# Triangular inverse of a gated DeltaNet layer: two chunks in each matmul, and two TensorE groups a level in place of three

## The chip, the cores and the metric

The kernel runs on one core of a Trainium2 chip. A core has TensorE (PE: matmuls from SBUF into PSUM), VectorE (DVE), ScalarE (ACT), GpSimd (POOL), SyncE (SP, which issues loads) and DMA queues. The engines run their own instruction streams and meet at semaphores. The metric is the device time of one execution in microseconds (us), lower is better.

## The reference, cut to what matters

One decoder layer on x of 1024 tokens by 1024 features, in float32: RMSNorm, one input projection, sliding-window attention (12 heads) beside a gated DeltaNet (8 heads of 128), sigmoid gates and an output projection, then a SwiGLU feed-forward. The change touches one step of the DeltaNet:

```
a = where(strict, beta_i * (k_i . k_j) * decay_ij, 0)      # strictly lower triangular, per chunk
sol = triangular_solve(eye + a, [beta * v, beta * exp(gc) * k], unit_diagonal)
u_bar, w = sol[..., :dv], sol[..., dv:]
# then a loop over the chunks that carries the state
```

The reference uses chunks of 64 tokens; the kernel uses eight chunks of 128 tokens, and forms the inverse of (eye + a) itself, which it then multiplies with both right-hand sides.

## The kernel before

**Dense stream.** The layer's projections are a long row of dense steps. `dense_k` (its matmul is line L198) issues three 128x512 matmuls for one slice of 128 input features, because each float32 operand is split into a high and a low part. A head's four projections (q, k, v, z) are 64 dense steps, numbered j = 0 to 63, sixteen for each weight tile. POOL splits a weight tile into its parts (L184, then L186) when the tile's slot is free, which is when PE has finished an earlier tile (steps 15, 31, 47, 63).

**Side steps.** The DeltaNet work of head h-1 is laid by hand between the dense steps of head h: `STEPS_AT` says after which dense step each piece is issued, and `delta_iteration` walks j on every engine, so that each engine has the same order. Seven such rounds run as a loop (`delta_heads`, heads 0 to 6 as side work); the eighth (`delta_end`) lies between the first 64 dense steps of the gates, whose outputs ACT takes with L920. On DVE the convolution of the next head's projections shares the round: `TAPS_AT` places its taps (`conv_vec`: L1458 for the first tap, L1460 for the others). ACT takes projection outputs into `conv_in` every eighth step (L1406) and applies SiLU at steps 30, 46 and 58 (`silu_delta_act`, L1416).

**The inverse.** `inv` holds, for each of eight chunks, the inverse of the diagonal blocks found so far; `inv_t` is its transpose, needed because the stationary operand of a matmul must be given transposed; `neg_a` is the masked minus a, transposed (the trace calls it `row`, by its buffer). Steps t00 and t01 (L1183) make the 2x2 blocks. Levels 1 to 6 double the block size, from 2 to 64 = 1 << level columns. A level has three steps, each in two halves of four chunks:

- y (L1194): for each chunk, neg_a times the left half-columns of `inv` (64 moving columns), into bank Y0 or Y1; ACT copies the result to `half_way` (L1292).
- d (L1204): for each chunk, inv times that (64 moving columns), into bank Z0 or Z1; DVE writes it into `inv` under a mask (L1357).
- t (L1210): for each chunk, a 128x128 transpose of `inv` into bank X0 or X1; ACT copies it to `inv_t` (L1295).

They follow steps 24 + 3 * (level - 1) and the two after it, so one dense step lies between every two groups on PE. A float32 matmul is two passes in the trace, so eight chunks in y or d are 16 rows of MATMUL; a transpose is one pass. At 42 come ub and wt (L1216, L1222), from 44 on the loop over the chunks, a0, b0, a1, b1 and so on, one piece a dense step (L1235, L1236 in a; L1240, L1241 in b; DVE L1370 and L1374 between them). At step 60 the decay rows of the next head are loaded, at 62 DVE prepares them.

Of the kernel before, what the change touches and what calls it, by code (L numbers as in the profile page):

```python
# [34 lines left out]
P = 128  # L35
# [30 lines left out]
def build(nc, x, norm_mix, w_in, conv_w, a_log, dt_bias, dn_norm, w_proj_attn, w_proj_delta,  # L66
          w_out, norm_ffn, w_gate, w_up, w_down, norm_final, out):
    ctx = ExitStack()
    with ctx:
# [1025 lines left out]
        col = dt_("col", [P, NCH, 4])  # L1095
        decay_all = dt_("decay_all", [P, NCH])
        state, u_now = dt_("state", [P, P]), dt_("u_now", [P, P])
        assert d0[0] <= work + 81920, d0[0] - work
        u_bar, w_t = inv, half_way
        o_raw, o_sq = beta_v, beta_k  # L1100

        dl = {x_: sem("dl_" + x_) for x_ in (
            "read", "conv", "silu", "sq", "ss", "ln", "normed", "vt", "bv", "kt", "kdec", "kk", "qk", "rows",
            "diff", "dec", "a", "pt", "t0t", "t0", "t0c", "y", "yc", "dt", "dtm", "tt", "ttc", "ub", "ubc", "wt", "wtc",
            "qdec", "ws", "u", "o", "s", "sup", "z", "os", "osq", "oss", "oln", "oexp", "out", "stored", "zero", "col", "eye")}

        def compact(t, c, level):

            return t[:, c * 64:(c + 1) * 64].rearrange("p (n b) -> p n b", b=1 << level)

        def c4(t, half):

# [2 lines left out]
        def chunk(t, c):  # L1115
            return t[:, c * P:(c + 1) * P]
# [1 line left out]


        STEPS_AT = {4: ["ss"], 8: ["vt0"], 9: ["vt1"], 15: ["kt0"], 16: ["kt1", "kk0"], 17: ["kk1"], 18: ["qk0"],  # L1120
                    19: ["qk1"], 21: ["t00"], 22: ["t01"], 42: ["ub0", "ub1", "wt0", "wt1"], 61: ["os"], 63: ["on"]}
        for level in range(1, 7):
            for n_, x_ in enumerate("ydt"):
                STEPS_AT[24 + 3 * (level - 1) + n_] = [f"{x_}{level}0", f"{x_}{level}1"]
        for c_ in range(NCH):
            STEPS_AT[44 + 2 * c_] = [f"a{c_}"]
            STEPS_AT[45 + 2 * c_] = [f"b{c_}"]

        WHOLE, HALVES = slice(0, S), (slice(0, HALF), slice(HALF, S))
        TAPS_AT = {20: (0, 0, WHOLE), 23: (0, 1, WHOLE), 25: (0, 2, WHOLE), 28: (0, 3, WHOLE),  # L1130
# [11 lines left out]
        def delta_pe(pe, h, step):  # L1142
# [35 lines left out]
            elif step[:2] == "t0":  # L1178
# [6 lines left out]
            elif step[0] in "ydt" and step[1] in "123456":  # L1185
                level, half = int(step[1]), int(step[2])
                n = h * 12 + (2 * (level - 1) + half)
                if step[0] == "y":
                    if level == 1:
                        pe.wait_ge(dl["t0c"], two + (half + 1))  # L1190
                        pe.wait_ge(dl["a"], two + 2)

                    for c in range(4 * half, 4 * half + 4):
                        last = mm(compact(bank[Y0 + half], c % 4, level), chunk(neg_a, c),  # L1194
                                  left(inv[:, :].rearrange("p (c t) -> p c t", t=P), level)[:, c], start=True, stop=True)
                    last.then_inc(dl["y"], 1)
                elif step[0] == "d":
                    pe.wait_ge(dl["yc"], n + 1)
                    if level > 1:
                        pe.wait_ge(dl["ttc"], n - 1)  # L1200
                    else:
                        pe.wait_ge(dl["pt"], two + (half + 1))
                    for c in range(4 * half, 4 * half + 4):
                        last = mm(bank[Z0 + half][:, (c % 4) * 64:(c % 4 + 1) * 64], chunk(inv_t, c),  # L1204
                                  half_way[:, c * 64:(c + 1) * 64], start=True, stop=True)
                    last.then_inc(dl["dt"], 1)
                else:
                    pe.wait_ge(dl["dtm"], n + 1)
                    for c in range(4 * half, 4 * half + 4):
                        last = tr(bank[X0 + half][:, (c % 4) * P:(c % 4 + 1) * P], chunk(inv, c), ident[:, :])  # L1210
                    last.then_inc(dl["tt"], 1)
            elif step[:2] == "ub":
                half = int(step[2])
                pe.wait_ge(dl["ttc"], h * 12 + (11 + half))
# [34 lines left out]
        def delta_act(act, h, step):  # L1249
# [33 lines left out]
            elif step[:2] == "t0":  # L1283
                half = int(step[2])
                act.wait_ge(dl["t0"], two + (half + 1))
                f(c4(inv, half), bank[X0 + half][:, :].rearrange("p (c t) -> p c t", t=P), ACT.Copy).then_inc(dl["t0c"], 1)
            elif step[0] in "yt" and step[1] in "123456":
                level, half = int(step[1]), int(step[2])
                n = h * 12 + (2 * (level - 1) + half)
                if step[0] == "y":  # L1290
                    act.wait_ge(dl["y"], n + 1)
                    f(half_way[:, half * 256:half * 256 + 256], bank[Y0 + half][:, 0:256], ACT.Copy).then_inc(dl["yc"], 1)  # L1292
                else:
                    act.wait_ge(dl["tt"], n + 1)
                    f(inv_t[:, half * HALF:(half + 1) * HALF], bank[X0 + half][:, :], ACT.Copy).then_inc(dl["ttc"], 1)  # L1295
            elif step[:2] == "ub":
                half = int(step[2])
                act.wait_ge(dl["ub"], two + (half + 1))
                f(u_bar[:, half * HALF:(half + 1) * HALF], bank[Y0 + half][:, :], ACT.Copy).then_inc(dl["ubc"], 1)
            elif step in ("b3", "b7"):  # L1300
                half = int(step[1]) // 4
                act.wait_ge(dl["o"], h * NCH + (4 * half + 4))

                f(o_raw[:, half * HALF:(half + 1) * HALF], bank[Y0 + half][:, :], ACT.Copy)
                f(o_sq[:, half * HALF:(half + 1) * HALF], bank[Y0 + half][:, :], ACT.Square).then_inc(dl["osq"], 1)
            elif step == "on":
                for half in range(2):
                    act.wait_ge(dl["oss"], two + (half + 1))
                    f(o_sq[:, half * HALF:(half + 1) * HALF], bank[Z0 + half][:, :], ACT.Ln, scale=1.0 / P,
                      bias=EPS).then_inc(dl["oln"], 1)  # L1310
                act.drain()
                f(o_sq[:, :], o_sq[:, :], ACT.Exp, scale=-0.5).then_inc(dl["oexp"], 1)

        def delta_vec(dve, h, step):
# [38 lines left out]
            elif step[0] == "d" and step[1] in "123456":  # L1353
# [70 lines left out]
        def prepare_vec(dve, h):  # L1424
# [15 lines left out]
            if isinstance(h, int):  # L1440

                v.tensor_copy(inv_t[:, :].rearrange("p (c t) -> p c t", t=P),
                              ident[:, :].unsqueeze(1).broadcast_to([P, NCH, P]))
            dve.drain()

        def conv_vec(dve, h, i, j, part):
# [540 lines left out]
```

## Time and profile before

| | |
|---|---|
| median of three runs | 2509.23 us (2508.02 to 2509.98) |
| span of the profiled execution | 2508.8 us |
| what lies around the span (median less span) | 0.4 us; the profiled execution has no time of its own on the page |
| busy PE, weight loads | 96%, 81% |
| busy DVE, ACT, POOL | 36%, 27%, 26% |
| chain that ended last | 87% PE, 5% DVE |
| one head's round (731.30 to 825.60 us) | 94.3 us, of which PE busy 93.37, DVE 45.90, ACT 42.60, POOL 13.71 |
| DMA in that round | 16% of the engines' time |

The busy shares of PE come from modelled ends: matmuls are pipelined and a row's duration is longer than the distance to the next row. So in what follows a group's cost on PE is read from the start of its first row to the start of the row behind it. The time stated behind a row as idle is likewise counted from the modelled end of the row ahead.

### The profile page before, as it was taken

The numbers are of one execution on the slowest core, as the hardware profiler recorded it, in microseconds if no ns is written. First come the engines' busy times: TensorE is split into PE (matmuls) and PEld (weight loads), VectorE is DVE, ScalarE is ACT, GpSimd is POOL, SyncE is SP. The second block draws the span as 40 slices with busy tenths as digits, with TensorE's granted clock in tenths as the row PEclk, the third lists the DMA queues.
The fourth block names the chain that finished last, engine by engine and source line by source line (L and its number), as shares of the span: only waits on it lengthen the run. The fifth ranks groups of instructions, "written<-read, shape, count | busy, mean of one in ns | idle before, by whom it ended". The sixth has DMA issues, their size and how long they took to land.

```text
span 2508.8 us, 33006 instructions
## 1 busy us (share of the span) xinstructions
PE 2417.1 (96%) x12464; PEld 2031.8 (81%) x12464; DVE 905.7 (36%) x1069; ACT 688.6 (27%) x1204; POOL 660.2 (26%) x447
## 2 busy tenths in 40 slices
PE   5999999999799999999999999999899999999998
PEld 4787878787788888888888888887788888888887
DVE  4416262627554454454453112321422112211234
ACT  4333232324343543543452320011211001100112
POOL 6242232212111111111111323333233233323321
PEclk9999999999899999999999999999999999999999
DMA  5112121213010210220220443332111111111112
GB/s 119 37 42 85 51 84 50 75 42 109 18 59 17 59 59 12 63 59 10 66 67 26 160 137 119 119 101 70 39 49 43 50 50 42 50 51 45 48 44 82
DMA packets 219108, 157.30 MB, mean 63 GB/s; under 512 B 22744, under 2 KB 205208, under 8 KB 217520
## 3 DMA queue, kind: packets, MB, share of 16 engines
q1 hardware_dynamic: 206528, 106.05, 15.1%
q10 hardware_dynamic: 12528, 50.53, 5.6%
q8 instruction: 35, 0.57, 0.1%
q14 instruction: 17, 0.14, 0.0%
HBM read 137.49 MB, written 19.07 MB: 62 GB/s over the span
## 4 chain that ended last, share of the span: by engine, by line
PE 87%; DVE 5%; DVEq 2%; DMA 2%; issue 1%; ACT 1%; POOL 1%; SPq 0%; ACTq 0%; POOLq 0%
PE bank L198 62%; PE bank L988 5%; PE bank L1194 3%; PE bank L1204 3%; PE bank L1210 2%; DVEq L765 1%; DMA stat_b<-scr_stat 1%; PE bank L1151 1%; PE bank L602 1%; PE bank L1235 1%; DVE joint L769 1%; PE bank L1170 1%; PE bank L1222 1%; PE bank L1216 1%; PE bank L1176 1%
## 5 line engine op out<-in xcount | busy, mean ns | idle before, releaser
L198 PE MATMUL bank<-u_hi,w_hi 128*128 128x512 f32 x2176 | 907.3, 417 | 16.2 <-DVE u_lo L1642 7.2
L198 PE MATMUL bank<-u_hi,w_lo 128*128 128x512 f32 x2176 | 852.7, 392 | 0.0
L198 PE MATMUL bank<-u_lo,w_hi 128*128 128x512 f32 x2176 | 850.5, 391 | 0.0
L184 POOL CAST w_hi<-raw 128x1024 fp32r<-128x1024 f32 (+1 forms) x176 | 183.6, 1043 | 1768.6 <-PE bank L198 1522.7
L198 PEld LDWEIGHTS bank<-u_hi,w_hi 128*128 128x128 f32 x2176 | 411.7, 189 | 91.6 <-DVE u_lo L1642 8.8
L198 PEld LDWEIGHTS bank<-u_hi,w_lo 128*128 128x128 f32 x2176 | 409.5, 188 | 88.5
L198 PEld LDWEIGHTS bank<-u_lo,w_hi 128*128 128x128 f32 x2176 | 412.2, 189 | 69.4 <-issue 3.8
L186 POOL TENSOR_TENSOR w_lo<-raw,w_hi 128x1024 fp32r<-128x1024 f32 (+1 forms) x176 | 430.9, 2448 | 25.7 <-issue 0.7
L1756 DVE TENSOR_TENSOR tmp<-tmp,bank 128x512 f32<-128x512 f32 x44 | 30.2, 687 | 367.0 <-PE bank L198 367.0
L198 PE MATMUL bank<-v_hi,w_hi 128*128 128x512 f32 x352 | 137.3, 390 | 2.6 <-DVE tmp L1756 2.6
L198 PE MATMUL bank<-v_hi,w_lo 128*128 128x512 f32 x352 | 137.0, 389 | 0.0
L198 PE MATMUL bank<-v_lo,w_hi 128*128 128x512 f32 x352 | 137.0, 389 | 0.0
L1728 ACT ACTIVATE tmp<-bank 128x512 f32<-128x512 f32 x44 | 26.4, 600 | 368.9 <-PE bank L198 368.8
L1357 DVE COPY_PREDICATED inv<-merge_mask,bank 128x256 f32<-128x256 uint8 x96 | 47.1, 491 | 221.9 <-PE bank L1204 221.9
L1460 DVE SCALAR_TENSOR_TENSOR conv_out<-conv_in,conv_c,conv_out 128x1024 f32<-128x1024 f32 (+1 forms) x96 | 102.2, 1065 | 15.0 <-issue 12.0
L1204 PEld LDWEIGHTS bank<-half_way,inv_t 128*128 128x128 f32 x768 | 93.1, 192 | 4.2
L1194 PEld LDWEIGHTS bank<-inv,row 128*128 128x128 f32 x768 | 93.1, 192 | 4.1
L1771 DVE TENSOR_TENSOR h_t<-h_t,bank 128x512 f32 x48 | 33.0, 687 | 162.2 <-PE bank L198 162.2
L1204 PE MATMUL bank<-half_way,inv_t 128*128 128x64 f32 x768 | 90.8, 272 | 0.0
L1194 PE MATMUL bank<-inv,row 128*128 128x64 f32 x768 | 90.8, 271 | 0.0
L1295 ACT ACTIVATE inv_t<-bank 128x512 f32<-128x512 f32 x96 | 52.2, 595 | 136.7 <-PE bank L1210 136.7
L1735 ACT ACTIVATE v_hi<-tmp 128x512 f32 (+1 forms) x44 | 27.8, 633 | 222.7 <-DVE tmp L1756 222.6
(238 smaller groups left out, 2792.4 us busy)
## 6 DMA issues: line engine op xcount, KB each, us to landing
raw<-in_w_in SPq DMA_DIRECT2D x84, 512.0 KB, 3.8
stat_b<-scr_stat ACTq DMA_DIRECT2D x12, 1024.0 KB, 6.7
row<-scr_rows ACTq DMA_DIRECT2D x24, 512.0 KB, 4.9
raw<-in_w_gate SPq DMA_DIRECT2D x22, 512.0 KB, 3.8
raw<-in_w_up SPq DMA_DIRECT2D x22, 512.0 KB, 3.9
scr_gate<-tmp ACTq DMA_DIRECT2D x16, 512.0 KB, 2.9
tmp<-scr_gate ACTq DMA_DIRECT2D x16, 512.0 KB, 4.2
raw<-in_w_down SPq DMA_DIRECT2D x16, 512.0 KB, 3.7
```

The source lines that it names most:

```text
L184: nc.gpsimd.tensor_copy(hi[:, 0:kt, :], raw[slot][:, 0:kt, :])
L186: nc.gpsimd.tensor_tensor(lo[:, 0:kt, :], raw[slot][:, 0:kt, :], hi[:, 0:kt, :].bitcast(F32), ALU.subtract).then_inc(weights_split, 1)
L198: last = nc.tensor.matmul(bank[dst][:, :], wpart[slot][wp][:, k, :], rhs[ap][:, k, half * HALF:(half + 1) * HALF], start=k == 0 and (wp, a ...
L988: last = nc.tensor.matmul(bank[dst][:, :], wpart[slot][wp][:, k, :], branch[ap][:, b, half * HALF:(half + 1) * HALF], start=start and (wp, ...
L1194: last = mm(compact(bank[Y0 + half], c % 4, level), chunk(neg_a, c), left(inv[:, :].rearrange("p (c t) -> p c t", t=P), level)[:, c], star ...
L1204: last = mm(bank[Z0 + half][:, (c % 4) * 64:(c % 4 + 1) * 64], chunk(inv_t, c), half_way[:, c * 64:(c + 1) * 64], start=True, stop=True)
L1210: last = tr(bank[X0 + half][:, (c % 4) * P:(c % 4 + 1) * P], chunk(inv, c), ident[:, :])
L1295: f(inv_t[:, half * HALF:(half + 1) * HALF], bank[X0 + half][:, :], ACT.Copy).then_inc(dl["ttc"], 1)
L1357: v.copy_predicated(left(c4(inv, half), level), left(merge_mask[:, level:level + 1, :].broadcast_to([P, 4, P]), level), bank[Z0 + half][:, ...
L1460: last = v.scalar_tensor_tensor(conv_out[:, part], shifted, tap, conv_out[:, part], ALU.mult, ALU.add)
L1756: v.tensor_tensor(tmp[1][:, hs], tmp[0][:, hs], bank[Y0 + half][:, :], ALU.mult).then_inc(ff["mult"], 1)
L1771: v.tensor_tensor(hf, hf, bank[OB[i][half]][:, :], ALU.add).then_inc(ff["added"], 1)
```

## The change

`half_pair`, `a_right` and `inv_right` are new buffers. Only half of a chunk's columns matter in a level: the left half-columns and the right half-columns of each block pair. The changed kernel packs the right columns of two chunks side by side, in `a_right` (from neg_a, by ACT) and in `inv_right` (from inv, by DVE, into 128x512 for all chunks). A y step is then four matmuls of 128 moving columns, each for two chunks; of its output only the two 64x64 diagonal blocks are used, which ACT copies in two pieces into `half_pair`, whose other blocks stay zero. The new step p transposes `inv_right` (four transposes) and ACT copies the result into the first half of `inv_t`. A d step contracts over the right columns of both chunks at once: four matmuls of 128 moving columns. y and p of a level are issued together, so a level has two groups with one dense step between. The full transpose of `inv` (tt) is made once, after level 6. The steps of the chunk loop move one dense step later. The diff's core, in this order: the table of steps, PE, ACT, DVE.

```diff
         STEPS_AT = {4: ["ss"], 8: ["vt0"], 9: ["vt1"], 15: ["kt0"], 16: ["kt1", "kk0"], 17: ["kk1"], 18: ["qk0"],
-                    19: ["qk1"], 21: ["t00"], 22: ["t01"], 42: ["ub0", "ub1", "wt0", "wt1"], 61: ["os"], 63: ["on"]}
+                    19: ["qk1"], 20: ["t00"], 21: ["t01"], 36: ["tt0", "tt1"], 39: ["ub0", "ub1", "wt0", "wt1"],
+                    62: ["os"], 63: ["on"]}
         for level in range(1, 7):
-            for n_, x_ in enumerate("ydt"):
-                STEPS_AT[24 + 3 * (level - 1) + n_] = [f"{x_}{level}0", f"{x_}{level}1"]
+            STEPS_AT[22 + 2 * (level - 1)] = [f"y{level}", f"p{level}"]
+            STEPS_AT[23 + 2 * (level - 1)] = [f"d{level}0", f"d{level}1"]
         for c_ in range(NCH):
-            STEPS_AT[44 + 2 * c_] = [f"a{c_}"]
-            STEPS_AT[45 + 2 * c_] = [f"b{c_}"]
+            STEPS_AT[45 + 2 * c_] = [f"a{c_}"]
+            STEPS_AT[46 + 2 * c_] = [f"b{c_}"]
...
+            elif step[0] == "y":
...
+                pe.wait_ge(dl["ar"], h * 6 + level)
+                for q in range(NCH // 2):
+                    if level > 1 and q % 2 == 0:
+                        pe.wait_ge(dl["dtm"], n + (q // 2 - 1))
+                    last = mm(by_block(chunk(bank[Y0], q), level), chunk(a_right, q),
+                              side_columns(inv[:, 2 * q * P:2 * (q + 1) * P], level, 0), start=True, stop=True)
+                last.then_inc(dl["y"], 1)
+            elif step[0] == "p":
+                level = int(step[1])
+                pe.wait_ge(dl["ir"], h * 6 + level)
+                for q in range(NCH // 2):
+                    last = tr(chunk(bank[X0], q), chunk(inv_right, q), ident[:, :])
+                last.then_inc(dl["pr"], 1)
+            elif step[0] == "d":
                 level, half = int(step[1]), int(step[2])
...
+                if half == 0:
+                    pe.wait_ge(dl["yc"], h * 6 + level)
+                    pe.wait_ge(dl["prc"], h * 6 + level)
...
+                for q in (2 * half, 2 * half + 1):
+                    last = mm(bank[Z0 + half][:, (q % 2) * P:(q % 2 + 1) * P], chunk(inv_t, q), half_pair[:, q, :],
+                              start=True, stop=True)
+                last.then_inc(dl["dt"], 1)
...
+                if half == 1:
+                    act.wait_ge(dl["a"], two + 2)
+                    f(by_block(a_right[:, :], 1), side_columns(neg_a[:, :], 1, 1), ACT.Copy).then_inc(dl["ar"], 1)
+            elif step[0] == "y":
+                level = int(step[1])
+                act.wait_ge(dl["y"], h * 6 + level)
+                y_now = bank[Y0][:, :].rearrange("p (q j) -> p q j", j=P)
+                f(half_pair[0:64, :, 0:64], y_now[0:64, :, 0:64], ACT.Copy)
+                f(half_pair[64:P, :, 64:P], y_now[64:P, :, 64:P], ACT.Copy).then_inc(dl["yc"], 1)
+                if level < 6:
+                    f(by_block(a_right[:, :], level + 1), side_columns(neg_a[:, :], level + 1, 1), ACT.Copy).then_inc(dl["ar"], 1)
+            elif step[0] == "p":
+                act.wait_ge(dl["pr"], h * 6 + int(step[1]))
+                f(inv_t[:, 0:HALF], bank[X0][:, :], ACT.Copy).then_inc(dl["prc"], 1)
...
+                if half == 1 and level < 6:
+                    dve.drain()
+                    v.tensor_copy(by_block(inv_right[:, :], level + 1),
+                                  side_columns(inv[:, :], level + 1, 1)).then_inc(dl["ir"], 1)
+            elif step == "t01":
+                dve.wait_ge(dl["t0c"], two + 2)
+                v.tensor_copy(by_block(inv_right[:, :], 1), side_columns(inv[:, :], 1, 1)).then_inc(dl["ir"], 1)
```

On PE, at level 2 of a head's loop round, the kernel before has this piece (L1194 is y, L1204 d, L1210 t, `row_140` is neg_a):

```order
L1194 MATMUL bank<-inv,row_140 128x64 x8
L198 MATMUL bank<-u_hi,w_hi_68 128x512
L198 MATMUL bank<-u_lo,w_hi_68 128x512
L198 MATMUL bank<-u_hi,w_lo_69 128x512
L1198 REGISTER_ALU
L1204 MATMUL bank<-half_way,inv_t 128x64 x4
L1198 REGISTER_ALU
L1204 MATMUL bank<-half_way,inv_t 128x64 x4
L198 MATMUL bank<-u_hi,w_hi_68 128x512
L198 MATMUL bank<-u_lo,w_hi_68 128x512
L198 MATMUL bank<-u_hi,w_lo_69 128x512
L1210 MATMUL bank<-ident,inv 128x128 x8
```

The changed kernel has this at the same level (L1203 is y, L1210 now p, L1220 d):

```order
L1199 REGISTER_ALU
L1202 REGISTER_ALU
L1203 MATMUL bank<-inv,a_right 128x128 x2
L1202 REGISTER_ALU
L1203 MATMUL bank<-inv,a_right 128x128 x2
L1210 MATMUL bank<-ident,inv_right 128x128 x4
L198 MATMUL bank<-u_hi,w_hi_68 128x512
L198 MATMUL bank<-u_lo,w_hi_68 128x512
L198 MATMUL bank<-u_hi,w_lo_69 128x512
L1220 MATMUL bank<-half_pair,inv_t 128x128 x4
```

Twenty-four matmuls and transposes a level have become twelve, and the dense step between d and the transposes is gone from here (it now lies behind level 6).

On ACT, around levels 4 and 5 of a loop round, the kernel before has this (L1292 copies y, L1295 the transposes, L1416 is the SiLU at step 30, L1406 takes a projection output):

```order
L1295 ACTIVATE inv_t<-bank 128x512 x2
L1291 REGISTER_ALU
L1292 ACTIVATE half_way<-bank 128x256
L1291 REGISTER_ALU
L1292 ACTIVATE half_way<-bank 128x256
L1411 REGISTER_ALU
L63 ISA
L1416 ACT_TABLE_LOAD
L1416 ACTIVATE qkv_129<-conv_out 128x1024
L1396 REGISTER_ALU
L1406 ACTIVATE conv_in_127<-bank 128x512
L1295 ACTIVATE inv_t<-bank 128x512 x2
```

The changed kernel has this there (L1311 and L1312 copy y, L1314 fills `a_right` for the next level, L1317 copies p, L1449 is the SiLU, L1439 takes the projection output; the last rows are level 6):

```order
L1311 ACTIVATE half_pair<-bank 64x4x64
L1312 ACTIVATE half_pair<-bank 64x4x64
L1314 ACTIVATE a_right<-row_140 128x512
L1317 ACTIVATE inv_t<-bank 128x512
L1444 REGISTER_ALU
L63 ISA
L1449 ACT_TABLE_LOAD
L1449 ACTIVATE qkv_129<-conv_out 128x1024
L1429 REGISTER_ALU
L1439 ACTIVATE conv_in_127<-bank 128x512
L1309 REGISTER_ALU
L1311 ACTIVATE half_pair<-bank 64x4x64
```

Four copies now stand in one queue between the y and the d of a level, where two stood between y and d and two between t and the next d.

On DVE, at levels 5 and 6 (L1383 writes `inv` under the mask, L1389 fills `inv_right` for the next level), the changed kernel has:

```order
L83 REGISTER_ALU
L1383 COPY_PREDICATED inv<-merge_mask,bank 128x8x32
L83 REGISTER_ALU
L1383 COPY_PREDICATED inv<-merge_mask,bank 128x8x32
L1389 COPY inv_right<-inv 128x512
L83 REGISTER_ALU
L1383 COPY_PREDICATED inv<-merge_mask,bank 128x4x64
```

The L1389 copy is new; before, the masked writes followed each other with only the convolution's taps between.

## Rows read from the trace of the kernel before

**Rows 1.** Waits of PE, 637 to 1391 us: engine, line, waited-for, total, times, longest (us)

```profile
PE bank L1165 <- DVE kn L1326: 13.5, 1, 13.5
PE bank L1235 <- DVE state L1374: 7.3, 9, 0.9
```

**Rows 2.** Timeline of PE, level 2: start (us), duration (us), line, matmul, tile shape, xcount

```profile
755.81 1.89 PE L1194 MATMUL bank<-inv,row 128*128 128x64 f32 x16
757.51 0.48 PE L198 MATMUL bank<-u_hi,w_hi 128*128 128x512 f32 x1
757.83 0.39 PE L198 MATMUL bank<-u_lo,w_hi 128*128 128x512 f32 x1
...
758.29 1.89 PE L1204 MATMUL bank<-half_way,inv_t 128*128 128x64 f32 x16
...
760.77 1.04 PE L1210 MATMUL bank<-ident,inv 128*128 128x128 f32 x8
...
762.34 0.33 PE L1194 MATMUL bank<-inv,row 128*128 128x64 f32 x2
```

**Rows 3.** Timeline of PE, groups of matmuls with 128 moving columns

```profile
742.45 1.05 PE L1176 MATMUL bank<-qn,kn 128*128 128x128 f32 x8
743.26 0.47 PE L198 MATMUL bank<-u_hi,w_hi 128*128 128x512 f32 x1
...
788.47 1.95 PE L1216 MATMUL bank<-beta_v,inv_t 128*128 128x128 f32 x16
790.26 1.95 PE L1222 MATMUL bank<-inv_t,beta_k 128*128 128x128 f32 x16
```

**Rows 4.** Timeline of ACT, copies from PSUM in the inverse and behind it

```profile
756.84 0.38 ACT L1292 ACTIVATE half_way<-bank 128x256 f32<-128x256 f32 x1 [0.88 <-PE bank L1194]
...
761.41 1.09 ACT L1295 ACTIVATE inv_t<-bank 128x512 f32<-128x512 f32 x2 [3.29 <-PE bank L1210]
...
789.56 0.60 ACT L1299 ACTIVATE inv<-bank 128x512 f32<-128x512 f32 x1 [0.94 <-PE bank L1216]
```

**Rows 5.** Timeline of DVE and PE, a place where PE waited

```profile
1363.56 0.29 DVE L1370 TENSOR_TENSOR u_now<-inv,bank 128x128 f32<-128x128 f32 x1
...
1363.91 0.49 PE L1240 MATMUL bank<-u_now,k_dec 128*128 128x128 f32 x2 [0.40 <-DVE u_now L1370]
...
1364.23 0.39 PE L1241 MATMUL bank<-row,u_now 128*128 128x128 f32 x2
```

**Rows 6.** Timeline of DVE: masked writes of levels 1 and 2, taps; POOL beside the long one

```profile
747.80 1.28 DVE L1460 SCALAR_TENSOR_TENSOR conv_out<-conv_in,conv_c,conv_out 128x1024 f32<-128x1024 f32 x1 [0.19 <-issue]
...
753.81 0.73 DVE L1357 COPY_PREDICATED inv<-merge_mask,bank 128x256 f32<-128x256 uint8 x1 [0.17 <-PE bank L1204]
...
759.44 0.43 DVE L1357 COPY_PREDICATED inv<-merge_mask,bank 128x256 f32<-128x256 uint8 x1 [3.41 <-PE bank L1204]
...
798.56 2.40 POOL L186 TENSOR_TENSOR w_lo<-raw,w_hi 128x1024 fp32r<-128x1024 f32 x1
...
798.91 2.35 DVE L1458 TENSOR_SCALAR conv_out<-conv_in,conv_c 128x512 f32<-128x512 f32 x1
...
801.43 0.47 DVE L1458 TENSOR_SCALAR conv_out<-conv_in,conv_c 128x512 f32<-128x512 f32 x1
```

**Rows 7.** Timeline of POOL, the split released by the end of dense step 31

```profile
765.16 1.04 POOL L184 CAST w_hi<-raw 128x1024 fp32r<-128x1024 f32 x1 [23.28 <-PE bank L198]
766.34 2.39 POOL L186 TENSOR_TENSOR w_lo<-raw,w_hi 128x1024 fp32r<-128x1024 f32 x1
```

**Rows 8.** Timeline of ACT, the SiLU of step 30 and the copy behind it

```profile
764.67 1.28 ACT L1416 ACT_TABLE_LOAD   x1
...
766.93 0.58 ACT L1406 ACTIVATE conv_in<-bank 128x512 f32<-128x512 f32 x1
```

**Rows 9.** Windows: stretch, us, PE and other busy us (instructions), PEclk, DMA share, GB/s

```profile
38.00:47.00 9.00, 6.11 (x34) 4.84 (x32) 4.93 (x6) 3.70 (x7) 8.05 (x7) 1.00 0.01 2
...
640.00:644.00 4.00, 3.21 (x12) 2.82 (x13) 3.16 (x4) 1.36 (x2) 0.00 (x0) 0.50 0.00 0
```

More of the change, by code:

```diff
@@ L1097, in build @@
         state, u_now = dt_("state", [P, P]), dt_("u_now", [P, P])
+        half_pair = dt_("half_pair", [P, NCH // 2, P])
+        a_right, inv_right = dt_("a_right", [P, HALF]), dt_("inv_right", [P, HALF])
         assert d0[0] <= work + 81920, d0[0] - work
@@ L1103, in build, with side_columns, by_block @@
             "read", "conv", "silu", "sq", "ss", "ln", "normed", "vt", "bv", "kt", "kdec", "kk", "qk", "rows",
-            "diff", "dec", "a", "pt", "t0t", "t0", "t0c", "y", "yc", "dt", "dtm", "tt", "ttc", "ub", "ubc", "wt", "wtc",
+            "diff", "dec", "a", "pt", "t0t", "t0", "t0c", "y", "yc", "ar", "ir", "pr", "prc", "dt", "dtm", "tt", "ttc", "ub", "ubc", "wt", "wtc",
             "qdec", "ws", "u", "o", "s", "sup", "z", "os", "osq", "oss", "oln", "oexp", "out", "stored", "zero", "col", "eye")}
-        def compact(t, c, level):
-            return t[:, c * 64:(c + 1) * 64].rearrange("p (n b) -> p n b", b=1 << level)
+        def side_columns(t, level, side):
+            return t.rearrange("p (m a b) -> p m a b", a=2, b=1 << level)[:, :, side, :]
+        def by_block(t, level):
+            return t.rearrange("p (m b) -> p m b", b=1 << level)
         def c4(t, half):
@@ L1184, in delta_pe @@
                 last.then_inc(dl["t0"], 1)
-            elif step[0] in "ydt" and step[1] in "123456":
-                level, half = int(step[1]), int(step[2])
[L1187 to L1211, printed above, removed]
@@ new lines, in delta_pe @@
+            elif step[0] == "y":
+                level = int(step[1])
+                n = h * 12 + 2 * (level - 1)
+                if level == 1:
+                    pe.wait_ge(dl["t0c"], two + 2)
+                    pe.wait_ge(dl["a"], two + 2)
+                pe.wait_ge(dl["ar"], h * 6 + level)
[12 more added lines that the diff above has]
+            elif step[0] == "d":
+                level, half = int(step[1]), int(step[2])
+                if half == 0:
+                    pe.wait_ge(dl["yc"], h * 6 + level)
+                    pe.wait_ge(dl["prc"], h * 6 + level)
+                if level == 1:
+                    pe.wait_ge(dl["pt"], two + (half + 1))
+                for q in (2 * half, 2 * half + 1):
+                    last = mm(bank[Z0 + half][:, (q % 2) * P:(q % 2 + 1) * P], chunk(inv_t, q), half_pair[:, q, :],
+                              start=True, stop=True)
+                last.then_inc(dl["dt"], 1)
+            elif step[:2] == "tt":
+                half = int(step[2])
+                pe.wait_ge(dl["dtm"], h * 12 + (11 + half))
+                for c in range(4 * half, 4 * half + 4):
+                    last = tr(bank[X0 + half][:, (c % 4) * P:(c % 4 + 1) * P], chunk(inv, c), ident[:, :])
+                last.then_inc(dl["tt"], 1)
@@ L1212, in delta_pe @@
             elif step[:2] == "ub":
                 half = int(step[2])
-                pe.wait_ge(dl["ttc"], h * 12 + (11 + half))
+                pe.wait_ge(dl["ttc"], two + (half + 1))
                 for c in range(4 * half, 4 * half + 4):
@@ L1286, in delta_act @@
                 f(c4(inv, half), bank[X0 + half][:, :].rearrange("p (c t) -> p c t", t=P), ACT.Copy).then_inc(dl["t0c"], 1)
[L1287 to L1295, printed above, removed]
+                if half == 1:
+                    act.wait_ge(dl["a"], two + 2)
+                    f(by_block(a_right[:, :], 1), side_columns(neg_a[:, :], 1, 1), ACT.Copy).then_inc(dl["ar"], 1)
+            elif step[0] == "y":
+                level = int(step[1])
+                act.wait_ge(dl["y"], h * 6 + level)
[7 more added lines that the diff above has]
+                f(inv_t[:, 0:HALF], bank[X0][:, :], ACT.Copy).then_inc(dl["prc"], 1)
+            elif step[:2] == "tt":
+                half = int(step[2])
+                act.wait_ge(dl["tt"], two + (half + 1))
+                f(inv_t[:, half * HALF:(half + 1) * HALF], bank[X0 + half][:, :], ACT.Copy).then_inc(dl["ttc"], 1)
             elif step[:2] == "ub":
@@ L1443, in prepare_vec @@
                               ident[:, :].unsqueeze(1).broadcast_to([P, NCH, P]))
+                v.memset(half_pair[:, :, :], 0.0)
             dve.drain()
```

## The prediction

> **What bounds the kernel now.** I read the page first, then the waits of PE, then the timeline of single levels on PE, ACT, DVE and POOL. PE is busy 96% of the span and makes up 87% of the chain that ended last. In the stretch with the DeltaNet heads its only waits of any size are one of 13.5 us ahead of the first round and nine of at most 0.9 us in the chunk loop [rows 1]; in the inverse it never waits. So a head's round lasts as long as what PE issues in it. Any PE work removed shortens the round, until an answer from ACT or DVE comes later than PE is ready for it. Both halves have to be priced.
>
> **What a level costs PE now.** Read from start to start [rows 2]: from the y of level 2 to the y of level 3 are 6.53 us. y takes 1.70 (755.81 to 757.51), the dense step behind it 0.78. From d to t are 2.48, the same again, and from t to the next y 1.57, so t takes 0.79. A dense step's first pass takes 0.32 behind a side group, the other two 0.23 each; away from groups I take three times 0.23, 0.70.
>
> **What a level costs PE after.** Eight passes of 128 moving columns took 0.81 when a dense step followed (742.45 to 743.26 [rows 3]). Sixteen took 1.79 when another group followed (788.47 to 790.26), 0.90 for eight. A pass of 64 columns took 0.106 (1.70 / 16), so doubling its columns costs nearly nothing, and halving the count is nearly all gain. Four transposes are half of 0.79, 0.40. A level is then y 0.90, p 0.40, dense 0.78, d 0.81, dense 0.78: 3.67 us. The dense step that left the level runs elsewhere for 0.70. Saved: 6.53 - 0.70 - 3.67 = 2.16 a level, 12.96 for six. The one full transpose, tt, with the longer first pass behind it, gives 0.87 back. That leaves 12.09 a head, 96.7 us for eight, if PE never waits.
>
> **The new waits.** d now needs both halves of y and the transposes, and all come through ACT in one queue. Count from the start of y. ACT began its copy of 789.56 1.09 after the group of 788.47 had started, which is eight passes [rows 3, 4]. A copy of 256 columns takes 0.38, a following one about 0.10 less (two of 512 columns took 1.09, one 0.60 [rows 4]). The copies of 64 partitions are not in the trace; since the time went with the columns, I take 0.28 each, no less than nothing and no more than 0.38. Filling `a_right` adds 0.49, the p copy 0.60, and PE starts 0.06 after what it waits for (1363.85 to 1363.91 [rows 5]). Sum: 1.09 + 0.28 + 0.28 + 0.49 + 0.60 + 0.06 = 2.80. PE is ready after 0.90 + 0.40 + 0.78 = 2.08, so it pauses 0.72. The pass after a pause is dearer: the pair there took 0.32 to the next line, against 0.22 for two passes in rows 3. With that 0.10 each of levels 1 to 5 loses 0.82. Level 6 fills no `a_right`: 2.31 against 2.08, 0.33 lost with the refill.
>
> The y of level 1 also waits for `a_right`. ACT starts a copy 0.64 after four transposes begin (760.77 to 761.41 [rows 2, 4]), then 0.49 and 0.60 and 0.06: 1.79. PE is ready after 0.40 + 0.78 = 1.18. Lost: 0.71 with the refill. Together 5 x 0.82 + 0.33 + 0.71 = 5.14 us a head.
>
> **The way back, through DVE.** The second masked write can start 1.09 after d and takes 0.45 (0.43 in [rows 6]), then 0.19 for the drain as ahead of the tap at 747.80, then the `inv_right` copy. Its nearest rows are a tap of 512 columns, 0.47, and the same tap at 2.35 [rows 6]. At 0.47 it ends 2.20 after d began, plus 0.10 refill, and p is due at 0.10 + 0.81 + 0.78 + 0.90 = 2.59: hidden. y's need of the masked writes (1.64 against 1.69) is just hidden too. At level 1 the masked write takes 0.73 (at 753.81), which moves p by some 0.2, behind ACT's longer chain. The taps stand behind the copy and are done before the next d.
>
> **One place where it is not hidden.** The tap of 2.35 began at 798.91 while POOL was in the L186 row of 798.56, and ended 0.30 after that one (801.26 against 800.96): a DVE instruction that reads one SBUF tensor stood still for POOL. The split that follows dense step 31 begins 0.34 after that step's end (762.34 + 2.48 = 764.82 to 765.16 [rows 2, 7]). In the changed order step 31 is the one ahead of d of level 5, whose DVE copy comes next. Count from the y of level 5: step 31 ends at 2.08, L186 runs from 3.60 to 5.99. d starts at 2.80, the copy wants to start at 4.63 and ends at 6.29. The p of level 6 was due at 5.39 and starts at 6.35, d of level 6 at 7.85 with its refill in place of 6.90. That is 0.95 a head.
> The Trainium skill (SBUF — State Buffer, Terms) says that DVE and GpSimd arbitrate for one port pair, held for a whole instruction, and that the loser fully blocks. By that rule the copy behind level 5 is blocked as worked out, and the traced tap agrees (2.35 us in place of 0.47); without it the sum would be 7.6 us lower.
>
> **What is free.** The SiLU of step 30 now stands behind p5 on ACT: from its table load to the end of the conv_in copy are 2.84 us [rows 8], and ACT's next copy is due 0.06 + 0.10 + 0.81 + 0.78 + 1.09 = 2.84 after p5's copy. If it were longer, level 6 would move by the difference. The chunk loop and ub move as a whole, with the same work around them. The load of the decay rows starts one dense step later, and DVE's preparation of them with it, behind which DVE waits for ACT's exponentials anyway. In `delta_end` there are neither taps nor SiLU, otherwise the same sum. The one memset of `half_pair` lies in the first preparation and costs at most a few tenths. The weights need 13.7 us of POOL in a round of 94, so a shorter round does not run into them.
>
> **Sum.** 8 x (12.09 - 5.14 - 0.95) = 48.0 us. From the span of 2508.8 that gives 2460.8; the median lies 0.4 above the span, so 2461.
>
> **Rivals.**
> *The copies cost more (2485).* `a_right` is read in runs of few columns. If ACT read these at half its rate, each of six fills would cost 0.49 more: 8 x 2.9 = 24 us. For it: the masked write of level 1, in runs of two, takes longer than the later ones. Against: ACT is another engine, and from level 2 on the runs are four and longer, where even DVE was at 0.43.
> *The waits hide (2412).* All 96.7 us arrive. It needs the ACT chain to be 0.7 us shorter than its copies' own durations allow. Only if some dense step were added between the groups.
> *The clock falls (2596, slower).* PE would pause in every level, some 0.8 of 4.5 us. After the wait of 13.5 us the clock was at 0.50 (640 to 644 us [rows 9]), 1.2 GHz. If the pauses held it there from y1 to d6, PE's own 6 x 3.67 = 22.0 us would double, less the 5.1 of pauses that then vanish: 8 x 17 = 135 us on top. It decides at a bit over a third of that stretch (48 / 135). Against: from 38 to 47 us PE was busy 6.11 of 9 us, less than it will be, and the granted clock was 1.00. The Trainium skill (TensorE: Matmul & The Clock Gate, A second HAM failure mode) tells of a kernel whose short idles between groups made the clock go to and fro; by that this rival holds, while our row of 38 to 47 us doesn't agree with it.
> *No change (2509).* The round is held by another chain, say projections, conv, SiLU, norm of one head ahead of kt of the next. Then PE would wait at L1165 for what it gains. Against: outside the first round PE never waits there, and most of that chain is itself paced by dense steps, which come sooner.
>
> **How the numbers follow.** My sum as it stands 0.70, dearer copies 0.14, hidden waits 0.06, a lower clock 0.05, no change 0.03, the rest unnamed. Within my sum: refills (6 us) and the collision (8 us) absent give 2447, and shorter 64-partition copies a few us more, 2440; the dearer copies close the other side, 2486. A measurement of this kernel tells changes above about 0.2%, 5 us. Faster by more 0.92, within 0.03, slower 0.05.
>
> **What would show it.** Right: PE matmuls of y and d in rows x8 with the next line 0.8 to 0.9 later; waits of PE for ACT ahead of d, five of about 0.6 idle in the record a head (the record counts from a modelled end, which hides some 0.16), one shorter; one ahead of y1; one for DVE ahead of p of level 6; a round of about 88.3 us; clock as before. Wrong: a y group of more than 1 us, `a_right` fills of about 1 us, PEclk below 0.9 in the inverse, or a wait at L1165's successor in every round.

## The result and the profile after

The changed kernel takes 2478.65 us (median of 4 runs, 2477.8 to 2479.46), the kernel before 2508.65 us (4 runs); the ratio is 0.9877, 95% interval 0.9863 to 0.9891. That is 30.0 us faster. Forecast were 2461 us, 48 us faster, with a range of 2440 to 2486.

The page of the changed kernel, busy time by engine and then the chain that ended last:

```profile
PE 2336.5 (94%) x11568; PEld 1934.3 (78%) x11568; DVE 927.9 (37%) x1118; ACT 702.0 (28%) x1220; POOL 659.0 (27%) x447
...
PE 84%; DVE 5%; ACT 3%; issue 3%; DVEq 2%; DMA 2%; POOL 1%; SPq 0%; ACTq 0%; POOLq 0%
```

PE issues 896 matmul rows fewer and is busy 80.6 us less (2417.1 before), but the span fell by 31.8 us only (2508.8 to 2477.0). ACT's share of the chain has risen from 1% to 3%. The waits of PE say where (same columns as [rows 1]):

```profile
PE bank L1220 <- ACT inv_t L1317: 34.8, 32, 1.1
PE bank L1172 <- DVE kn L1352: 17.4, 1, 17.4
PE bank L1220 <- issue: 8.4, 8, 1.1
...
PE bank L1257 <- DVE u_now L1403: 6.8, 9, 0.9
...
PE bank L1203 <- ACT a_right L1306: 4.5, 8, 0.6
...
PE bank L1210 <- DVE inv_right L1389: 2.0, 8, 0.3
```

L1220 is d. It waits 32 + 8 = 40 times, which is five levels in eight heads; the eight put down to issue are those of level 1. L1203 <- a_right is the y of level 1, L1210 <- inv_right the p of level 6. The wait in the chunk loop (L1257) has the size it had before under another line. The one ahead of the first round (L1172) is 17.4 us in place of 13.5, but that costs nothing: it ends at 640.55 against 640.79, PE only came to it earlier.

The timeline of PE, levels 3 and 6 of the second round, which answers to [rows 2] (L1203 y, L1210 p, L1227 the full transpose):

```profile
754.63 1.05 PE L1203 MATMUL bank<-inv,a_right 128*128 128x128 f32 x8
755.53 0.60 PE L1210 MATMUL bank<-ident,inv_right 128*128 128x128 f32 x4
757.91 1.13 PE L1220 MATMUL bank<-half_pair,inv_t 128*128 128x128 f32 x8 [1.09 <-ACT inv_t L1317]
759.58 1.05 PE L1203 MATMUL bank<-inv,a_right 128*128 128x128 f32 x8
...
769.48 1.05 PE L1203 MATMUL bank<-inv,a_right 128*128 128x128 f32 x8
770.79 0.66 PE L1210 MATMUL bank<-ident,inv_right 128*128 128x128 f32 x4 [0.25 <-DVE inv_right L1389]
772.22 1.13 PE L1220 MATMUL bank<-half_pair,inv_t 128*128 128x128 f32 x8
775.27 1.03 PE L1227 MATMUL bank<-ident,inv 128*128 128x128 f32 x8
```

y takes 0.90 and d with its dense step 1.67, as priced with the restart behind a pause. But d starts 3.28 after y, where 2.80 was forecast. The level lasts 4.95 us in place of 4.49. ACT in the same level:

```profile
755.73 0.38 ACT L1311 ACTIVATE half_pair<-bank 64x256 f32<-64x256 f32 x1 [2.90 <-PE bank L1203]
756.12 0.38 ACT L1312 ACTIVATE half_pair<-bank 64x256 f32<-64x256 f32 x1
756.52 0.63 ACT L1314 ACTIVATE a_right<-row 128x512 f32<-128x512 f32 x1
757.17 0.60 ACT L1317 ACTIVATE inv_t<-bank 128x512 f32<-128x512 f32 x1
```

The copies follow each other at 0.39, 0.40 and 0.65 us, not at 0.28, 0.28 and 0.49: none overlaps the one ahead. From the end of the last (757.77) to d are 0.14, not 0.06.

The y of level 2 is dearer than that of level 3: 1.06 (749.52 to 750.58) where 0.90 was priced. The code makes each half of it wait for one of DVE's two masked writes of the level before, and those of level 1 take longer than later ones:

```profile
748.66 1.31 DVE L1383 COPY_PREDICATED inv<-merge_mask,bank 128x256 f32<-128x256 uint8 x2 [4.34 <-PE bank L1220]
...
749.52 1.22 PE L1203 MATMUL bank<-inv,a_right 128*128 128x128 f32 x8
...
753.81 0.87 DVE L1383 COPY_PREDICATED inv<-merge_mask,bank 128x256 f32<-128x256 uint8 x2 [1.82 <-PE bank L1220]
```

The writes of level 1 end at 749.97, 0.45 behind the start of the y that needs them; those of level 2 end at 754.68, 0.05 behind the start of theirs, whose second half doesn't come to wait.

**The account of a head.** y of level 1 starts 0.66 late (forecast 0.61 ahead of the refill). From y of level 1 to y of level 6 pass 25.01 us (744.47 to 769.48) against 5 x 3.67, 6.66 lost (forecast 4.10, with the 0.10 of the restart at level 1 counted to its y). In level 6, y to d takes 2.74 against 2.08, 0.66 lost, and 0.08 more for the refill, the dearer first passes behind a pause (forecast 0.33 + 0.95). Together 8.06, forecast 6.09. So a head saves 12.09 - 8.06 = 4.03, 32 us for eight. In the timelines the last matmul of the eighth chunk loop starts at 1346.34 against 1379.94, 33.6 us earlier. Behind it the span is 1.8 us longer (1130.7 against 1128.9), where the code is the same. The granted clock differs there: from 2458.9 to 2465.7 PE was busy throughout at 0.50 in the changed kernel, and at the same place of the kernel before it had 1.00. So these 1.8 us are most likely the clock in this one execution and not the change; no run isolates them.

### The profile page after: what moved, and what is told of

Same layout as the page of the kernel before. It is cut to its first block, busy times and chain, and to the rows that moved or that the text cites. A ratio compares the mean times of both kernels' runs of the same rounds, so it can differ in the third digit from the quotient of the medians.

```text
span 2477.0 us, 31268 instructions
## 1 busy us (share of the span) xinstructions
PE 2336.5 (94%) x11568; PEld 1934.3 (78%) x11568; DVE 927.9 (37%) x1118; ACT 702.0 (28%) x1220; POOL 659.0 (27%) x447
## 4 chain that ended last, share of the span: by engine, by line
PE 84%; DVE 5%; ACT 3%; issue 3%; DVEq 2%; DMA 2%; POOL 1%; SPq 0%; ACTq 0%; POOLq 0%
PE bank L198 62%; PE bank L988 5%; PE bank L1220 2%; PE bank L1203 2%; DMA stat_b<-scr_stat 1%; PE bank L1158 1%; DVEq L765 1%; PE bank L602 1%; ACT inv_t L1317 1%; ACT a_right L1314 1%; PE bank L1257 1%; PE bank L613 1%; PE bank L1177 1%; PE bank L1239 1%; PE bank L1233 1%
## 5 line engine op out<-in xcount | busy, mean ns | idle before, releaser
L1220 PEld LDWEIGHTS bank<-half_pair,inv_t 128*128 128x128 f32 x384 | 46.5, 191 | 63.3 <-issue 63.3
L1383 DVE COPY_PREDICATED inv<-merge_mask,bank 128x256 f32<-128x256 uint8 x96 | 45.6, 492 | 134.0 <-PE bank L1220 133.7
L1220 PE MATMUL bank<-half_pair,inv_t 128*128 128x128 f32 x384 | 54.2, 284 | 43.8 <-ACT inv_t L1317 34.8
L1795 DVE TENSOR_TENSOR v_lo<-tmp,v_hi 128x512 f32 (+1 forms) x44 | 83.5, 1933 | 0.1
L198 PEld LDWEIGHTS bank<-v_hi,w_hi 128*128 128x128 f32 x352 | 66.1, 188 | 17.5 <-issue 3.8
L660 ACT ACTIVATE prob<-score,neg_max 128x256 f32<-128x256 f32 (+1 forms) x96 | 44.5, 465 | 116.5 <-DVE neg_max L722 111.0
```

The lines of the kernel that those rows point to most:

```text
L198: last = nc.tensor.matmul(bank[dst][:, :], wpart[slot][wp][:, k, :], rhs[ap][:, k, half * HALF:(half + 1) * HALF], start=k == 0 and (wp, a ...
L660: last = nc.scalar.activation(prob[p % 2][:, i * w:(i + 1) * w], score[p % 2][:, i * w:(i + 1) * w], ACT.Exp, bias=neg_max[:, b:b + 1], ac ...
L1220: last = mm(bank[Z0 + half][:, (q % 2) * P:(q % 2 + 1) * P], chunk(inv_t, q), half_pair[:, q, :], start=True, stop=True)
L1383: v.copy_predicated(left(c4(inv, half), level), left(merge_mask[:, level:level + 1, :].broadcast_to([P, 4, P]), level), bank[Z0 + half][:, ...
L1795: v.tensor_tensor(v_region[1][:, ds(j, 1), hs].rearrange("p a t -> p (a t)"), tmp[1][:, hs], v_region[0][:, ds(j, 1), hs].rearrange("p a t ...
```

## The experiments

All times stand against the kernel before in the same session.

**The fill of a_right behind p's copy.** ACT only:

```diff
             elif step[0] == "y":
...
-                if level < 6:
-                    f(by_block(a_right[:, :], level + 1), side_columns(neg_a[:, :], level + 1, 1), ACT.Copy).then_inc(dl["ar"], 1)
             elif step[0] == "p":
...
                 f(inv_t[:, 0:HALF], bank[X0][:, :], ACT.Copy).then_inc(dl["prc"], 1)
+                level = int(step[1])
+                if level < 6:
+                    f(by_block(a_right[:, :], level + 1), side_columns(neg_a[:, :], level + 1, 1), ACT.Copy).then_inc(dl["ar"], 1)
```

> ACT fills a_right for the next level behind the copy of p, no longer ahead of it. Theory A (PE's pauses ahead of d are the queue of copies on ACT, each copy at its full length: 1.10 + 0.39 + 0.40 + 0.65 + 0.60 + 0.14 = 3.28 us from y to d): the 0.65 us of the fill leaves the sum, y to d becomes 2.63 in levels 1 to 5, 5 x 0.65 x 8 = 26 us are gained; at level 6 the inv_right copy now wants to start earlier, still ends with POOL's split, and gives some 0.4 us a head back: about 2456 us. Theory B (the pause is not ACT's queue, but for instance the masked writes on DVE or the weight load's own lateness): y to d stays 3.28 and the time stays 2478.

Measured: 2457.82 us, ratio 0.9796 (0.9779 to 0.9812). PE, levels 4 and 6:

```profile
754.80 1.05 PE L1203 MATMUL bank<-inv,a_right 128*128 128x128 f32 x8
...
757.42 1.13 PE L1220 MATMUL bank<-half_pair,inv_t 128*128 128x128 f32 x8 [0.43 <-ACT inv_t L1315]
...
763.39 1.05 PE L1203 MATMUL bank<-inv,a_right 128*128 128x128 f32 x8
765.34 0.66 PE L1210 MATMUL bank<-ident,inv_right 128*128 128x128 f32 x4 [0.90 <-DVE inv_right L1390]
```

y to d is 2.62, so the wait is the queue on ACT: Theory A. And the p of level 6 now comes 1.95 after its y, where 1.31 were needed in the changed kernel. The collision with POOL's split, DVE and POOL there:

```profile
763.54 1.74 DVE L1390 COPY inv_right<-inv 128x512 f32<-128x512 f32 x1
...
762.63 2.37 POOL L186 TENSOR_TENSOR w_lo<-raw,w_hi 128x1024 fp32r<-128x1024 f32 x1
```

In the changed kernel the same pair reads:

```profile
768.07 2.37 POOL L186 TENSOR_TENSOR w_lo<-raw,w_hi 128x1024 fp32r<-128x1024 f32 x1
...
769.64 1.09 DVE L1389 COPY inv_right<-inv 128x512 f32<-128x512 f32 x1
```

In the other levels the copy takes 0.43. Here it ends 0.28 and 0.29 after POOL does, wherever it began: its length is set by the end of POOL's row. By the rule of the Trainium skill (SBUF — State Buffer, Terms: the loser fully blocks) that is as it should be.

**Two dense steps between y and d.** The levels take three steps again, ACT as in the changed kernel:

```diff
-            STEPS_AT[22 + 2 * (level - 1)] = [f"y{level}", f"p{level}"]
-            STEPS_AT[23 + 2 * (level - 1)] = [f"d{level}0", f"d{level}1"]
+            STEPS_AT[22 + 3 * (level - 1)] = [f"y{level}", f"p{level}"]
+            STEPS_AT[24 + 3 * (level - 1)] = [f"d{level}0", f"d{level}1"]
```

and tt goes to 41, ub and wt to 43.

> Two dense steps between the y/p group and d of a level, one between d and the next y (levels every third step again), ACT's order as in the changed kernel. Theory A: PE is ready for d at 2.78 instead of 2.08 us, the answer still comes at 3.28, so 0.70 us less pause in levels 1 to 5, none at level 6, the collision with POOL's split gone: about 8 x 4.2 = 33 us, 2445 us. Theory B (the missing gain is PE's own: the new matmuls or the clock cost more than priced): the pauses shrink but the groups lengthen, and the time stays near 2478.

Measured: 2445.04 us, ratio 0.9749 (0.9733 to 0.9766). A level on PE:

```profile
753.15 1.05 PE L1203 MATMUL bank<-inv,a_right 128*128 128x128 f32 x8
...
756.43 1.13 PE L1220 MATMUL bank<-half_pair,inv_t 128*128 128x128 f32 x8 [0.40 <-ACT inv_t L1317]
...
758.10 1.05 PE L1203 MATMUL bank<-inv,a_right 128*128 128x128 f32 x8
```

y to d is 3.28 as in the changed kernel and the level 4.95, but now with three dense steps in it. Moving a dense step costs PE nothing, and it fills 0.7 us of a wait that is there anyway. Theory A: 2445 us were expected.

**When the copies don't overlap.** Four edits of ACT's copies in the changed kernel, all else as it is. First, whole 128-partition copies of two 128-column blocks:

```diff
-                f(half_pair[0:64, :, 0:64], y_now[0:64, :, 0:64], ACT.Copy)
-                f(half_pair[64:P, :, 64:P], y_now[64:P, :, 64:P], ACT.Copy).then_inc(dl["yc"], 1)
+                f(half_pair[:, 0:2, :], y_now[:, 0:2, :], ACT.Copy)
+                f(half_pair[:, 2:4, :], y_now[:, 2:4, :], ACT.Copy).then_inc(dl["yc"], 1)
```

> The two copies of y into half_pair take 128 partitions by two 128-column blocks each, instead of 64 partitions by four 64-column blocks; same number of elements in a partition. The unused blocks of half_pair then hold values that are not zero, so the output is another one. Theory A (an ACT copy overlaps the one before by 0.10 us only where it spans all partitions): starts 0.29 instead of 0.39 apart, up to 0.2 us less in each of six levels, 2469 us. Theory B (the overlap is lost for another reason): starts 0.39 apart as now, 2478 us.

Measured: 2464.85 us, ratio 0.9825 (0.9809 to 0.9842), 13.8 us below the changed kernel, more than the 9 expected. ACT:

```profile
754.08 0.38 ACT L1311 ACTIVATE half_pair<-bank 128x256 f32<-128x256 f32 x1 [2.90 <-PE bank L1203]
754.36 0.38 ACT L1312 ACTIVATE half_pair<-bank 128x256 f32<-128x256 f32 x1
754.62 0.63 ACT L1314 ACTIVATE a_right<-row 128x512 f32<-128x512 f32 x1
755.14 0.60 ACT L1317 ACTIVATE inv_t<-bank 128x512 f32<-128x512 f32 x1
```

Distances 0.28, 0.26, 0.52: the overlap is back between all three pairs, the fill and p's copy included, which nobody had touched. PE starts d 2.89 after y (752.99 to 755.88) in place of 3.28.

Second, the fill reads 512 columns in a row:

```diff
-                    f(by_block(a_right[:, :], level + 1), side_columns(neg_a[:, :], level + 1, 1), ACT.Copy).then_inc(dl["ar"], 1)
+                    f(a_right[:, :], neg_a[:, 0:HALF], ACT.Copy).then_inc(dl["ar"], 1)
```

> The fills of a_right of levels 2 to 6 read 512 columns of neg_a in a row instead of blocks of 4 to 64 columns, so the values and the output are others. Theory A (reading in blocks makes the copy longer, 0.63 instead of 0.60, and keeps the next copy from overlapping): 0.13 us less in levels 1 to 5, 5 us, 2473 us. Theory B (the blocks don't matter): the same 0.65 from start to start, 2478 us.

Measured: 2477.15 us, ratio 0.9878 (0.9862 to 0.9895). The fill still takes 0.63 and p's copy follows at 0.65 or 0.66 us. Reading in blocks of 4 columns and more costs nothing (the first fill of a head, in blocks of 2, is not changed here; it takes 0.66): Theory B, and with it the rival of dearer copies falls in the form in which the prediction had it.

Third, strided blocks but all partitions (one execution):

```diff
+                f(half_pair[:, :, 0:64], y_now[:, :, 0:64], ACT.Copy)
+                f(half_pair[:, :, 64:P], y_now[:, :, 64:P], ACT.Copy).then_inc(dl["yc"], 1)
```

> The two copies of y keep their four blocks of 64 columns at a stride, but take all 128 partitions each; the unused blocks of half_pair then hold values that are not zero, so the output is another one. Theory A (the overlap was lost to the 64 partitions): starts 0.28 apart and the next one 0.26, as with the full-partition copies of whole blocks, 2465 us. Theory B (it was lost to the strided blocks): 0.39 apart as in the changed kernel, 2478 us.

Measured: 2467.6 us in one run, distances 0.28, 0.26 and 0.53 (754.90, 755.18, 755.44, 755.97). So it isn't the blocks that cost the overlap, it is the partitions.

Fourth, the two 64-partition copies in the other order (one execution):

```diff
+                f(half_pair[64:P, :, 64:P], y_now[64:P, :, 64:P], ACT.Copy)
+                f(half_pair[0:64, :, 0:64], y_now[0:64, :, 0:64], ACT.Copy).then_inc(dl["yc"], 1)
```

> The two 64-partition copies of y are issued in the other order (upper partitions first). Theory A (a copy of 64 partitions lets nothing overlap its end, wherever it stands): starts 0.39 and 0.40 apart as in the changed kernel, 2478 us. Theory B (only a copy that starts at partition 64, or the step from one half to the other, costs the overlap): one of the two distances falls to 0.29.

Measured: 2470.3 us in one run. ACT, with the upper partitions in L1311:

```profile
754.97 0.38 ACT L1311 ACTIVATE half_pair<-bank 64x256 f32<-64x256 f32 x1 [2.90 <-PE bank L1203]
755.36 0.38 ACT L1312 ACTIVATE half_pair<-bank 64x256 f32<-64x256 f32 x1
755.64 0.62 ACT L1314 ACTIVATE a_right<-row 128x512 f32<-128x512 f32 x1
756.16 0.58 ACT L1317 ACTIVATE inv_t<-bank 128x512 f32<-128x512 f32 x1
```

Theory A falls. Theory B's sign came, one of the two distances is 0.28, but neither of its two reasons alone gives both orders: the first distance stays at 0.39, and the two behind it fall to 0.28 and 0.52. So between a lower-half and an upper-half copy there is no overlap in either order, and the copies behind lose theirs only when the upper-half copy came last. Why the fill and p's copy, two instructions later, are touched by that stays open: with the fill out of the way (first experiment) p's copy starts 0.40 behind the upper-half copy, but the fill behind it overlaps again (756.68 to 757.17). In which part of ACT this happens, no run shows.

**The waits covered.** The two dense steps, the late fill, and the first fill of a head moved ahead of the t0 copies:

```diff
                 half = int(step[2])
+                if half == 0:
+                    act.wait_ge(dl["a"], two + 2)
+                    f(by_block(a_right[:, :], 1), side_columns(neg_a[:, :], 1, 1), ACT.Copy).then_inc(dl["ar"], 1)
                 act.wait_ge(dl["t0"], two + (half + 1))
                 f(c4(inv, half), bank[X0 + half][:, :].rearrange("p (c t) -> p c t", t=P), ACT.Copy).then_inc(dl["t0c"], 1)
-                if half == 1:
-                    act.wait_ge(dl["a"], two + 2)
-                    f(by_block(a_right[:, :], 1), side_columns(neg_a[:, :], 1, 1), ACT.Copy).then_inc(dl["ar"], 1)
```

> Three moves together: two dense steps between the y/p group and d (as in e2), the fill of a_right behind the copy of p (as in e1), and the first fill of a head ahead of the t0 copies, where ACT was idle. Theory A (all that the change lost against the 96.7 us of PE work is waits for copies): y to d needs 2.63 us and PE is ready at 2.78, y of level 1 doesn't wait either; from the 2445 us of e2 go 5 x 0.58 x 8 = 23 us and 0.75 x 8 = 6 us, 2416 us, within 5 us of 2508.5 - 96.7 = 2412. Theory B (part of the loss is PE's own, dearer matmuls or a lower clock behind the pauses): the waits vanish and the time stays 10 us or more above 2412.

Measured: 2418.74 us (5 runs), ratio 0.964 (0.9627 to 0.9654), the fastest kernel of the study, 59.9 us below the changed one. Levels 3 and 4 on PE:

```profile
743.57 0.60 PE L1210 MATMUL bank<-ident,inv_right 128*128 128x128 f32 x4
745.40 1.05 PE L1220 MATMUL bank<-half_pair,inv_t 128*128 128x128 f32 x8
746.99 1.05 PE L1203 MATMUL bank<-inv,a_right 128*128 128x128 f32 x8
747.88 0.60 PE L1210 MATMUL bank<-ident,inv_right 128*128 128x128 f32 x4
749.96 1.13 PE L1220 MATMUL bank<-half_pair,inv_t 128*128 128x128 f32 x8
```

The d of level 3 follows its p by 1.83, four transposes and two dense steps, with nothing waited for. The d of level 4 comes 0.25 later in the loop rounds: ACT is still busy with the SiLU of step 30 and the conv_in copy behind it, so its copies of that y start late. The level takes 4.63 in place of 4.31, 7 x 0.32 = 2.2 us. What is gained against the kernel before is 91.0 us; with those 2.2 it is 93.2, of the 96.7 priced as PE work. Two small waits are left in every head besides. The y of level 1 starts at 733.73, 0.24 late, because it needs ACT's copy of the last t0 transposes (ended 733.60), and its restart costs 0.12; the y of level 2 loses 0.18 to the masked writes of level 1, as in the changed kernel. Together 0.54 a head, some 4 us, about as much as is missing. The time is 7 us above Theory A's 2412, outside its 5, and below the 10 of Theory B; with these waits named it is Theory A, and PE's own terms were right to within a few us.

**Three groups a level.** As the last, but p behind a dense step of its own:

```diff
-            STEPS_AT[22 + 3 * (level - 1)] = [f"y{level}", f"p{level}"]
+            STEPS_AT[22 + 3 * (level - 1)] = [f"y{level}"]
+            STEPS_AT[23 + 3 * (level - 1)] = [f"p{level}"]
```

> As e5, but p stands behind a dense step of its own: three groups of half the size a level, each behind one dense step, as in the kernel before. This is the packing of two chunks alone, without the merging of two groups. Theory A: p's result now reaches ACT at 1.59 + 0.64, is copied at 2.83 and reaches PE at 2.97 us, where PE is ready at 2.73: a pause of 0.24 + 0.08, and 0.08 more for one more return to dense steps, 0.40 x 6 x 8 = 19 us over e5, 2435 us. Theory B (it is the count of passes alone that matters, the order of the groups is free): the time of e5 within 5 us.

Measured: 2431.35 us, ratio 0.9682 (0.9667 to 0.9697), 12.6 us over the kernel with two groups and the waits covered. A level from the third on takes 4.62 to 4.65 us in place of 4.31 (here L1204 is y, L1211 p, L1221 d):

```profile
749.97 1.13 PE L1221 MATMUL bank<-half_pair,inv_t 128*128 128x128 f32 x8
751.63 1.05 PE L1204 MATMUL bank<-inv,a_right 128*128 128x128 f32 x8
753.22 0.60 PE L1211 MATMUL bank<-ident,inv_right 128*128 128x128 f32 x4
754.62 1.13 PE L1221 MATMUL bank<-half_pair,inv_t 128*128 128x128 f32 x8
```

The direction is Theory A's, the size two thirds of it: the pause is there (y to d 2.99, forecast 2.97), but the further 0.08 a level for one more return to dense steps is not, and level 4 had lost its 0.32 already. So packing two chunks into a matmul, with this placing of the groups, brings 78 us of the 91, and joining y with p the other 13. In the changed kernel, whose groups are joined with only one dense step between, 30 of them arrive.

## Why the prediction was right in its range and high in its gain

**The bound.** Right: PE's issue sets the round, and of 96.7 us of PE work removed 91.0 come out as time once nearly nothing is waited for.

**PE's terms** (2.16 us a level, 12.09 a head, 96.7 in all). Right: y 0.90, d with its dense step 1.59 and 1.67 behind a pause; p took 0.36 where 0.40 was taken. The prediction had named a y group of more than 1 us as a sign of being wrong, and the y of levels 1 and 2 did take 1.02 and 1.06; but these are a restart behind a pause and a wait for the masked writes, not dearer matmuls, since the same matmuls take 0.89 from level 3 on. The kernel with covered waits gains 91.0.

**The ACT chain** (2.80 us from y to d). This is the step that failed, in size: it measured 3.28. Of the 0.48, 0.11 and 0.12 are the two half_pair copies, taken at 0.28 and measured 0.39 and 0.40; 0.16 is the fill, taken at 0.49 and measured at 0.65; 0.08 is PE's start behind ACT, 0.14 for 0.06; 0.01 is ACT's own start. The sentence that was wrong is that a following copy takes 0.10 less: read from copies of 128 partitions, carried over to copies of 64. I had named 0.38 as the upper bound there and not used it for the fill, to which the loss spreads. A level loses 1.28 for 0.82 by it (4.95 against 3.67), and five levels times eight heads times 0.46 us are 18.4 us, as much as the whole miss of 18.0. The other terms nearly cancel: level 6 lost 4.3 us less than forecast, the y of level 2 cost 1.3 and that of level 1 0.4 more, and 2.2 lie outside the heads.

**The collision with POOL.** The mechanism was right, the size was off for the changed kernel: it depends on how late d of level 5 is. There p of level 6 came 0.41 late, since the longer ACT chain had delayed d; with the chain short, as I had assumed it, 1.05 (first experiment), forecast 0.96 from 5.39 to 6.35. It returned part of the miss: level 6 lost 0.74 in place of 1.28. That is one error making up for a part of another, not foresight.

**The y of level 1.** 0.66 late, forecast 0.61.

**What was costed at nothing.** Held with two exceptions. The y's need of the masked writes was called just hidden, and the longer write of level 1 was followed to p but not to the y of level 2, which loses up to 0.18 us a head by it. And the copy behind the SiLU of step 30, just hidden in the prediction, costs 0.32 a round where the ACT chain no longer hides it (in the kernel with covered waits).

**The rivals.** The dearer copies came true in effect but not by their mechanism; reading in blocks of 4 columns and more is free. The hidden waits need the dense step between the groups, as the prediction said, but not it alone: with it a wait of 0.40 a level was left (second experiment), which the late fill took away. The clock did not fall: in a stretch of the changed kernel with five pauses PE was busy 21.88 of 28 us at 1.00, which is 2.4 GHz, while after the long wait ahead of the first round it was at 0.50, 1.2 GHz (columns as in [rows 9]):

```profile
640.00:644.00 4.00, 3.45 (x13) 3.06 (x14) 3.08 (x5) 0.58 (x1) 0.00 (x0) 0.50 0.00 0
744.00:772.00 28.00, 21.88 (x145) 18.26 (x145) 11.80 (x19) 14.93 (x28) 3.41 (x2) 1.00 0.00 1
```

So the row of 38 to 47 us in [rows 9] was the better guide, for pauses of this size. The Trainium skill (TensorE: Matmul & The Clock Gate, A second HAM failure mode) tells of a clock that goes to and fro under short idles between groups; this trace doesn't show that in the inverse.

**Around the span.** The profiled execution of the changed kernel took 2478.76 us with a span of 2477.0; what lies around it is 1.8 us, not the 0.4 read from a median and another run's span. The other side agrees: a run of the kernel before with the span of 2508.8 took 2510.51. So the profiled execution of the kernel before was some 2 us slower than the median of 2508.65, and the spans differ by 31.8 us where the medians differ by 30.0.

## What to carry to other kernels

When side work is laid between steps of a dense stream, joining groups takes cover away (here one dense step a level of three): count, for each group, the answers of the other engines end to end against the dense work up to the next group, and move dense steps to where that sum is longer, since they cost the same anywhere. Put copies that nothing waits for behind those that release the bound engine. And price copies in a queue at their full length unless the trace has the same pair.

## What the runs showed of the hardware that was not expected

- ACT copies of 256 columns follow each other at 0.28 us when both span 128 partitions, at 0.39 when one is on partitions 0 to 63 and the other on 64 to 127, in either order. Behind a last copy on the upper half the next two distances are 0.40 and 0.65 when the fill of `a_right` comes next, 0.40 and 0.49 when the copy of p does; behind one on the lower half 0.28 and 0.52 (one execution).
- Two passes of a float32 matmul with 64 moving columns took 0.21 us, with 128 columns 0.20 to 0.22: the 64 columns fewer saved nothing. The prediction had read this from the rows, and the changed kernel bears it out.
- A DVE copy of one SBUF tensor (0.43 us) that meets POOL's tensor_tensor ends 0.28 us after it, whenever it began: 1.09, 1.38 and 1.74 us long in three kernels. The two masked writes just ahead of it, which read PSUM and a mask in SBUF, lay wholly beside the same row of POOL in the changed kernel (768.65 to 769.55) and took 0.90 us together, as against 0.87 to 0.89 without it.
- PE took up work 0.06 us after a result of DVE and 0.13 to 0.14 us after one of ACT.
